# The attention loop of a two-block kernel: maxima by pieces, transposes and value product a step later, the projection begun around the loop's end

## The reference

```python
def diff_attention(q, k_all, v_all, lam):
    s = jnp.einsum('bhmqd,bhmkd->bhmqk', q, k_all).astype(jnp.float32) * ATTN_SCALE
    pr = jax.nn.softmax(s, axis=-1)
    a = pr[:, :, 0] - lam * pr[:, :, 1]
    return jnp.einsum('bhqk,bhke->bhqe', a.astype(v_all.dtype), v_all)

def diff_post(o, p, lam_init):
    o = rmsnorm(o, p['subln_w'], SUBLN_EPS) * (1.0 - lam_init)
```

## Time and profile before

| | |
|---|---|
| Median of three runs | 3520.77 us (3517.88 to 3523.02) |
| Profiled execution | span 3522.8 us, 57651 instructions |
| PE, DVE, ACT busy | 3351.5, 1923.6, 947.3 us (95%, 55%, 27%) |
| Mean granted TensorE clock | 0.977 of full speed |
| Softmax stage, first scores to spill landed | 248.9 to 510.4 us |
| Project stage from | 510.6 us |

### The profile page before, as it was taken

How to read it: one execution, slowest core, us unless ns; L and a number is a source line. 1 busy time by engine, 2 the same in 40 slices (tenths; PEclk the granted TensorE clock), 3 DMA queues, 4 the chain that set the end, 5 groups by cost and what they waited for, 6 DMA issues and landing times.

```text
span 3522.8 us, 57651 instructions
## 1 busy us (share of the span) xinstructions
PE 3351.5 (95%) x25613; PEld 2091.0 (59%) x25613; DVE 1923.6 (55%) x3171; ACT 947.3 (27%) x1914; POOL 51.0 (1%) x117
## 2 busy tenths in 40 slices
PE   7998879989999998989999999999999999999998
PEld 3446655558989887444444444445566447777853
DVE  2137744547767676645655640126988765434524
ACT  3246641115454554211000000100111413233310
POOL 2000000000000000000000000000000000000000
PEclk8999989989989999999999999999999999999999
DMA  6010002300000001232111121113011111100021
GB/s 242 0 55 1 1 25 90 131 30 7 15 18 4 3 3 63 80 102 72 66 49 35 45 98 42 55 48 110 13 52 38 55 66 54 36 24 25 1 90 66
DMA packets 110572, 177.18 MB, mean 50 GB/s; under 512 B 5427, under 2 KB 66482, under 8 KB 109682
## 3 DMA queue, kind: packets, MB, share of 16 engines
q1 hardware_dynamic: 101682, 144.67, 12.1%
q10 hardware_dynamic: 8640, 28.82, 2.4%
HBM read 147.26 MB, written 26.21 MB: 49 GB/s over the span
## 4 chain that ended last, share of the span: by engine, by line
PE 84%; DVE 9%; ACT 4%; DMA 2%; issue 1%; POOL 0%; ACTq 0%; DVEq 0%; SPq 0%; POOLq 0%
PE psum_all L66 82%; ACT sbuf_all L72 3%; DVE sbuf_all L91 3%; DVE sbuf_all L99 2%; DVE sbuf_all L81 2%; PE psum_all L111 1%; ACT L72 1%; DMA sbuf_all<-in_x 1%; DVE sbuf_all L105 1%; DMA sbuf_all<-in_w_out 0%; DVE sbuf_all L88 0%; DMA sbuf_all<-in_w_up 0%; POOL sbuf_all L81 0%; DVE sbuf_all L111 0%; DMA yd_spill<-sbuf_all 0%
## 5 line engine op out<-in xcount | busy, mean ns | idle before, releaser
L66 PE MATMUL psum_all<-sbuf_all 64*64 64x64 f32 (+8 forms) x24858 | 3253.0, 317 | 129.4 <-ACT sbuf_all L72 61.6
L66 PEld LDWEIGHTS psum_all<-sbuf_all 64*64 64x64 f32 (+2 forms) x24858 | 2006.6, 155 | 1351.8 <-issue 966.8
L72 ACT ACTIVATE sbuf_all<-psum_all 128x256 f32<-128x256 f32 (+6 forms) x889 | 363.4, 426 | 1395.5 <-PE psum_all L66 1252.8
L91 DVE SCALAR_TENSOR_TENSOR sbuf_all<-sbuf_all 128x520 f32<-128x520 f32 (+8 forms) x783 | 581.0, 776 | 16.9
L81 DVE TENSOR_TENSOR sbuf_all<-sbuf_all 128x512 f32<-128x512 f32 (+12 forms) x559 | 460.4, 848 | 172.4 <-ACT sbuf_all L72 128.9
L72 ACT ACTIVATE sbuf_all<-sbuf_all 128x64 f32<-128x64 f32 (+16 forms) x539 | 306.7, 581 | 822.6 <-DVE sbuf_all L75 348.6
L75 DVE COPY sbuf_all<-psum_all 128x256 f32<-128x256 f32 (+6 forms) x141 | 72.5, 524 | 456.7 <-PE psum_all L66 430.5
L72 ACT ACTIVATE sbuf_all<-psum_all,sbuf_all 128x1280 f32<-128x1280 f32 (+5 forms) x212 | 164.2, 780 | 312.4 <-PE psum_all L66 273.9
L81 DVE TENSOR_TENSOR sbuf_all<-sbuf_all,psum_all 128x512 f32<-128x512 f32 (+2 forms) x160 | 101.9, 639 | 250.4 <-PE psum_all L66 249.1
L105 DVE COPY_PREDICATED sbuf_all<-sbuf_all,psum_all 128x256 f32<-128x256 int32 (+2 forms) x296 | 143.9, 490 | 68.0 <-PE psum_all L66 62.4
L87 DVE TENSOR_SCALAR sbuf_all<-sbuf_all 128x256 f32<-128x256 f32 (+9 forms) x151 | 57.6, 419 | 163.2 <-ACT sbuf_all L72 160.0
(11 more groups left out here) (21 smaller groups left out, 167.4 us busy)
## 6 DMA issues: line engine op xcount, KB each, us to landing
sbuf_all<-in_w_mod SPq DMA_DIRECT2D x12, 2048.0 KB, 8.0
sbuf_all<-in_w_up SPq DMA_DIRECT2D x22, 1024.0 KB, 7.7
sbuf_all<-in_w_in SPq DMA_DIRECT2D x6, 2048.0 KB, 9.2
x_spill<-sbuf_all SPq DMA_DIRECT2D x16, 512.0 KB, 2.9
sbuf_all<-in_conv_w_in SPq DMA_DIRECT2D x16, 512.0 KB, 5.2
sbuf_all<-in_gla_w_in SPq DMA_DIRECT2D x8, 1024.0 KB, 5.2
sbuf_all<-in_w_down SPq DMA_DIRECT2D x4, 1792.0 KB, 7.5
hid_spill<-sbuf_all ACTq DMA_DIRECT2D x9, 512.0 KB, 2.6
```

Of the source, the lines that this page charges most:

```text
L66: return self.e.matmul(out, lhsT, rhs, start=start, stop=stop, skip_group_check=True)
L72: return self.e.activation(out, in_, func, bias=bias, scale=scale, **kw)
L91: return self.e.scalar_tensor_tensor(out, a, s, b, op0, op1) if self.e is not None else Unissued()
```

## The change

In the softmax stage:

- Scores of both maps lie side by side in PSUM columns 0 to 2559, five banks; bank 5 holds the third transposed group and the value product, banks 6 and 7 the first two groups. The six score matmuls come in the order D, A, E, C, F, B, one signal each. C shares bank 2 with D and waits for it.
- The maxima are taken by these pieces, in the order A, E, D, C, F, B, with a maximum over three values at the end of each map. Map 1 is done first and exponentiated first.
- The transposes are those of step n - 2 and the value product that of step n - 3, and the product comes first. Probabilities of map 0 have three buffers, the transposed ones a single one. ScalarE makes all three copies; VectorE none.
- VectorE does the maxima of step n ahead of the combination of step n - 1. Mean and scalings of a head come four steps later, and all head transposes and outputs leave the loop: five of eight go to TensorE's step 32, three into project_tensor.
- project_tensor waits neither for the end of the softmax stage nor for the spill. It runs head transposes, low-rank products and the last value product in turns. The other engines wait as before.

The diff, with most of the removed lines left out, since they stand above:

```diff
@@ -577,15 +577,16 @@
-    K.pbuf = [[sb.take(ALL) for m in range(2)] for _ in range(2)]
-    K.pT = [sb.take(ALL) for _ in range(2)]
-    K.stats = sb.take(16)
+    K.p0, K.p1 = [sb.take(ALL) for _ in range(3)], [sb.take(ALL) for _ in range(2)]
+    K.pT = sb.take(ALL)
+    K.stats = sb.take(4 * 16)
-    K.small = K.slots([K.ps[:, i * BANK:(i + 1) * BANK] for i in (6, 7)])
-    K.scores = [K.ps[:, 0:ALL], K.ps[:, 3 * BANK:3 * BANK + ALL]]
-    K.score_done = [K.new_signal(f"softmax_score{m}_done") for m in range(2)]
+    K.scores = [K.ps[:, 0:ALL], K.ps[:, ALL:2 * ALL]]
+    K.turn_bank = {0: K.ps[:, 6 * BANK:7 * BANK], 4: K.ps[:, 7 * BANK:8 * BANK], 8: K.ps[:, 5 * BANK:5 * BANK + 256]}
+    K.weigh_bank = K.ps[:, 5 * BANK + 256:5 * BANK + 384]
+    K.score_done = K.new_signal("softmax_score_done")
...
@@ -701,6 +702,15 @@
+SCORES = {"D": (1, 0, 256), "A": (0, 0, 512), "E": (1, 256, 768), "C": (0, 1024, ALL), "F": (1, 768, ALL), "B": (0, 512, 1024)}
+TOPS = (("A", "A", 3), ("E", "E", 0), ("D", "C", 1), ("C", "C", 4), ("F", "F", 2), ("B", "B", 5))
+def softmax_stats(K, n):
+    return K.stats[:, 16 * (n % 4):16 * (n % 4) + 16]
...
@@ -711,52 +721,66 @@
         if n:
             te.wait_ge(*A.s.by("exp", n - 1, 0))
             te.wait_ge(*A.s.by("exp", n - 1, 1))
...
+        for part, (m, a, b) in SCORES.items():
+            rows = slice(m * HEAD, (m + 1) * HEAD)
+            if part == "C":
+                te.wait_ge(*K.score_done.by(n, "D"))
+            te.matmul(K.scores[m][:, a:b], K.q[rows, h, i * P:(i + 1) * P],
+                      K.k[rows, h, a:b]).then_inc(*K.score_done.tick(n, part))
+    def turns(n):
         te.wait_ge(*A.v.by("combined", n))
...
+        for g, bank in K.turn_bank.items():
+            w = min(4, 10 - g)
+            if n:
+                te.wait_ge(*A.s.by("turned", n - 1, g))
+            for kk in range(w):
+                done = te.transpose(bank[:, kk * P:(kk + 1) * P], K.p0[n % 3][:, (g + kk) * P:(g + kk + 1) * P], K.ident)
+            done.then_inc(*A.t.tick("turns", n, g))
     def weigh(n):
         h, i = WORK[n]
...
+        te.wait_ge(*(A.s.by("weighed", n - 1) if n else A.s.by("lam_exp")))
+        te.wait_ge(*A.s.by("turned", n, 8))
+        product(te, K.weigh_bank, lambda kk: pT[:, kk * P:(kk + 1) * P], lambda kk: v[:, kk, h * P:(h + 1) * P],
                 10).then_inc(*A.t.tick("weigh", n))
...
+    last = len(WORK) - 1
+    for n in range(last + 3):
+        if n <= last:
             scores(n)
         if n == 0:
             te.wait_ge(*A.v.by("lam_products"))
...
+            te.matmul(K.weigh_bank[:, 0:2], K.ones, K.lam[:, 0:2]).then_inc(*A.t.tick("lam"))
+        if n > 2:
+            weigh(n - 3)
         if n > 1:
...
+            turns(n - 2)
+        if n == last + 1:
+            te.wait_ge(*A.s.by("exp", last, 0))
+            te.wait_ge(*A.s.by("exp", last, 1))
+            K.bank.turn = -1
+            for x in range(5):
+                turn_head(K, te, *divmod(x, 2))
+def turn_head(K, te, h, g):
+    A = K.softmax
+    te.wait_ge(*A.v.by("normed", h, g))
+    bank = open_bank(K, te, "yd", h, g)
+    for i in range(4):
+        done = te.transpose(bank[:, i * P:(i + 1) * P], K.o_rows[:, h, 4 * g + i, :], K.ident)
+    done.then_inc(*A.t.tick("yd", h, g))
+def last_weigh(K, te):
+    A, n = K.softmax, len(WORK) - 1
+    te.wait_ge(*A.s.by("weighed", n - 1))
+    te.wait_ge(*A.s.by("turned", n, 8))
+    product(te, K.weigh_bank, lambda kk: K.pT[:, kk * P:(kk + 1) * P], lambda kk: K.v[:, kk, 3 * P:4 * P],
+            10).then_inc(*A.t.tick("weigh", n))
 def softmax_vector(K, ve):
@@ -773,37 +797,29 @@
         ve.tt(neg_lam, lam[:, 3:4], lam[:, 2:3], ALU.subtract).then_inc(*V.tick())
         ve.wait_ge(*V.now())
         ve.ts(neg_lam, neg_lam, -LAM_INIT, ALU.add).then_inc(*V.tick())
+    def tops(n):
+        s_ = softmax_stats(K, n)
+        for part, written, col in TOPS:
+            m, a, b = SCORES[part]
+            ve.wait_ge(*K.score_done.by(n, written))
+            ve.reduce(s_[:, col:col + 1], K.scores[m][:, a:b], ALU.max).then_inc(*V.tick())
+            if part in "FB":
+                at = 3 - 3 * m
+                ve.wait_ge(*V.now())
+                ve.reduce(s_[:, 6 + m:7 + m], s_[:, at:at + 3], ALU.max, negate=True).then_inc(*V.tick("top", n, m))
+    def combine(n):
+        s_ = softmax_stats(K, n)
+        ve.wait_ge(*A.s.by("exp", n, 0))
+        ve.wait_ge(*A.s.by("exp", n, 1))
+        if n >= 4:
+            ve.wait_ge(*A.s.by("weighed", n - 4))
+        ve.recip(s_[:, 10:12], s_[:, 8:10]).then_inc(*V.tick())
         ve.wait_ge(*V.now())
...
+        ve.stt(s_[:, 12:13], s_[:, 11:12], neg_lam, s_[:, 8:9], ALU.mult, ALU.mult).then_inc(*V.tick())
         ve.wait_ge(*V.now())
...
+        ve.stt(K.p0[n % 3], K.p1[n % 2], s_[:, 12:13], K.p0[n % 3], ALU.mult, ALU.add).then_inc(*V.tick("combined", n))
     def head_mean(h):
         ssq = K.ssq[:, h * NT:(h + 1) * NT]
...
@@ -822,27 +838,25 @@
     def head_out(h, g):
         ve.wait_ge(*A.t.by("yd", h, g))
-        ve.ts(K.q[:, h, g * 512:(g + 1) * 512], K.small.view("yd", h, g), K.col["subln_w"], ALU.mult, 1.0 - LAM_INIT,
+        ve.ts(K.q[:, h, g * 512:(g + 1) * 512], K.bank.view("yd", h, g), K.col["subln_w"], ALU.mult, 1.0 - LAM_INIT,
               ALU.mult).then_inc(*V.tick())
-        K.small.end(("yd", h, g), V.now())
+        K.bank.end(("yd", h, g), V.now())
     for n in range(len(WORK) + 1):
-        h, step = n // 8 - 1, n % 8
+        h, step = (n - 12) // 8, (n - 12) % 8
+        if n < len(WORK):
+            tops(n)
         if n == 1:
             negative_lam()
+            ve.wait_ge(*V.now())
         if n:
             combine(n - 1)
-        if h >= 0 and step in (5, 6):
-            head_out(h, step - 5)
-        if n < len(WORK):
-            top(n, 0)
-            top(n, 1)
-        if n:
-            turned(n - 1, 8)
-        if h >= 0 and step == 2:
+        if h >= 0 and step == 0:
             head_mean(h)
-        if h >= 0 and step in (3, 4):
-            head_rows(h, step - 3)
+        if h >= 0 and step in (1, 2):
+            head_rows(h, step - 1)
+    for x in range(6):
+        head_out(*divmod(x, 2))
     head_mean(3)
     for g in range(2):
         head_rows(3, g)
@@ -856,33 +870,33 @@
     for s in K.heads_.ends():
         se.wait_ge(*s)
     se.wait_ge(*A.t.by("lam"))
...
+    se.activation(K.lam[:, 2:4], K.weigh_bank[:, 0:2], ACT.Exp).then_inc(*S.tick("lam_exp"))
     def exp(n, m):
...
+        s_ = softmax_stats(K, n)
         se.wait_ge(*A.v.by("top", n, m))
...
+        if m == 0 and n >= 3:
+            se.wait_ge(*A.t.by("turns", n - 3, 8))
+        if m == 1 and n >= 2:
             se.wait_ge(*A.v.by("combined", n - 2))
...
+        to = K.p1[n % 2] if m else K.p0[n % 3]
+        se.activation(to, K.scores[m], ACT.Exp, bias=s_[:, 6 + m:7 + m], accum=s_[:, 8 + m:9 + m]).then_inc(*S.tick("exp", n, m))
+    def turned(n):
+        if n:
+            se.wait_ge(*A.t.by("weigh", n - 1))
+        for g, bank in K.turn_bank.items():
+            w = min(4, 10 - g)
+            se.wait_ge(*A.t.by("turns", n, g))
+            se.activation(K.pT[:, g * P:(g + w) * P], bank, ACT.Copy).then_inc(*S.tick("turned", n, g))
     def weighed(n):
         h, i = WORK[n]
...
         o = K.o_rows[:, h, i, :]
         se.wait_ge(*A.t.by("weigh", n))
...
+        if n + 1 < len(WORK):
+            se.wait_ge(*A.t.by("turns", n + 1, 8))
+        se.activation(o, K.weigh_bank, ACT.Copy, scale=softmax_stats(K, n)[:, 10:11]).then_inc(*S.tick("weighed", n))
         se.wait_ge(*S.now())
         se.activation(K.sq_junk, o, ACT.Square, accum=K.ssq[:, h * NT + i:h * NT + i + 1]).then_inc(*S.tick("squared", n))
@@ -891,20 +905,18 @@
         se.wait_ge(*A.v.by("mean_square", h))
         se.activation(ssq, ssq, ACT.Sqrt).then_inc(*S.tick("root", h))
-    for n in range(len(WORK) + 2):
-        if 0 < n <= len(WORK):
-            turned(n - 1, 0)
-            turned(n - 1, 4)
+    for n in range(len(WORK) + 4):
+        if 3 <= n < len(WORK) + 3:
+            turned(n - 3)
+        if n >= 4:
+            weighed(n - 4)
         if n < len(WORK):
+            exp(n, 1)
             exp(n, 0)
-            exp(n, 1)
-        if n > 1:
-            weighed(n - 2)
-        if n >= 10 and n % 8 == 2:
-            head_root(n // 8 - 1)
+        if n >= 12 and n % 8 == 4 and n < len(WORK) + 1:
+            head_root(n // 8 - 1 if n < 36 else 3)
     head_root(3)
-    for s in (A.t.final(), A.v.final()):
-        se.wait_ge(*s)
+    se.wait_ge(*A.v.final())
     se.dma_start(K.yd_dram, K.q).then_inc(*K.dma("spill_yd").tick())
@@ -940,8 +952,6 @@
 def project_tensor(K, te):
     J, hT = K.project, K.hT
-    for s in (*K.softmax.ends(), K.dma("spill_yd").final()):
-        te.wait_ge(*s)
     def turn_values(j):
         te.wait_ge(*J.v.by("conv", 2, j))
@@ -962,11 +972,25 @@
         done.then_inc(*J.t.tick("mod_sum", block))
```

(22 more changed lines are left out.)

77 lines of the change are left out of this document (removed).

## The result

| | before | after |
|---|---|---|
| Median, timed side by side | 3521.89 us (4 runs, 3517.88 to 3525.95) | 3489.85 us (4 runs, 3488.88 to 3495.29) |
| Ratio | | 0.9909, 95% interval 0.9895 to 0.9922 |
| Span of the profiled execution | 3522.8 us | 3493.1 us |

A forecast was written before the change was run, and what follows sets the result against it. It took TensorE, busy for 95% of 3522.8 us, as the bound, so time saved ahead of the projection counts. Loop 5.7 plus tail 10.1 made 15.8 us, giving 3505.0 us against the median; range 3497 to 3516.

The forecast's parts named there:

- The ring of the step: Attention loop: chain from scores through maxima and exponentials back to scores, forecast at 7.07 us a step instead of 7.11.
- exponentials 1.53 + 1.42: Loop step on ScalarE: 1.53 us from first exponential to second, then 1.42 to the accumulator read.
- 0.15 to TensorE: End of the loop step: 0.15 us from ScalarE's accumulator read to TensorE's next scores.
- lower bound for the step: Attention loop: cheapest case, small maximum 0.05 less and A ready at 0.95, giving a step of 6.9 us.
- Heads: Loop steps that carry a head's end: 2.5 us extra for three heads where 7.0 were, a gain of 4.5.
- Start: Slow first three steps of the loop: 3.0 us extra left as before, between 1 and 5.
- The tail: From last scores to low-rank products done: 54.8 us against 64.9, 10.1 earlier.
- Pieces at full hand-over: Maxima in the loop: each piece costs the full 0.11 us hand-over, step 7.84, program 3529 us; 5%.
- Less overlap: Maxima in the loop: pieces overlap by 0.03 us instead of 0.08, program 3511 us; 14%.
- Scores in strict order: Score matmuls in the loop run in program order, A ready 0.15 us later each step, program 3510 us; 5%.
- Hidden tail: Projection keeps its old end as TensorE meets late copies or sums; only the loop's 5.7 us left, 3515 us; 8%.
- The case without low clock: No low clock in the tail and a start of 1 us, program 3500.5 us; 15%.

The follow-up runs named there:

- b_bothtops: The kernel before, with the first exponential made to wait for both maxima; 3564.49 us.
- b_onewait: The kernel before, with a step's scores waiting only for the second exponential (map 1) of the step before; 3513.5 us.
- a_twowait: The kernel after, with scores waiting for the exponentials in the order they are made (map 1, then map 0), so the second is its own wait; 3502.33 us.
- a_again: The kernel after once more, unchanged; 3491.29 us.
- b_nospill: The kernel before, with TensorE's part of the projection not waiting for the landing of the spill; 3516.03 us.
- a_combfirst: The kernel after, with VectorE doing the combination of step n - 1 ahead of the maxima of step n; 3512.57 us.
- a_oldtail: The kernel after, with low-rank products beginning only when the whole softmax stage has ended and the spill has landed; 3506.41 us.
- a_shift7: The kernel after, with a 512-column low-rank product at the start of the projection done twice; 3507.74 us.
- a_whole: The kernel after, with one whole maximum per map instead of pieces, both exponentials waiting for both; 3566.32 us.

## Why the prediction was wrong in size

**The ring of the step: right in structure, two terms mis-sized.** Up to the first exponential the working holds to 0.03: A ready early, pieces 0.61 and 0.33 apart (five from 375.80 to the small maximum at 378.38), small maximum, hand-over. The failed terms are the last two. "exponentials 1.53 + 1.42" took a start-to-start time of ScalarE from a place where it ended on a wait; 1.32 is the pace (b_bothtops). "0.15 to TensorE" took a hand-over with two waits for one that the change made single; it is 0.05 (b_onewait, a_twowait). In the sum the first term is 0.21 too long and the second 0.10. With 0.03 and 0.01 from the rest that is 0.35 a step, 31 x 0.35 = 10.9 us; the start below takes 1.9 of it back and the heads give 0.2: 9.2. Its lower bound for the step, 6.9, varied only the pieces and didn't hold the 6.72.

**Heads: right.** 7.50 for a long step, +0.78 each for three, 2.3 where 2.5 were forecast.

**Start: 3.0 us forecast, 4.9 measured** (215.5 - 31 x 6.72 - 2.3). From 248 to 283 us the granted clock is 0.90 in before, 0.76 in this profile of after and 0.90 in a_again, whose loop is 2.1 us shorter: the size lies within what one kernel shows from run to run.

**The tail: right in sum, the reason half right.** 54.4 for 54.8. But I spread the gain over work drawn forward, and b_nospill's tail gets nearly all of it from the one wait for the spill. The late spill cost TensorE nothing: ScalarE stood idle for 14 us ahead of its first low-rank copies at 505.31, and TensorE never waited for them.

**The rest:** 0.9 from the opening and 3.4 behind the projection, both in unchanged code. Both stretches differ between two profiles of the same kernel too: a_again has its first exponential 1.3 later than after, and takes 1.2 less behind the mark, a part that took from 2805 to 2823 us in these kernels. No run ties these 4.3 us to the change. I had left them out and had no range for them. Together 9.2 + 0.4 + 0.9 + 3.4 = 13.9, which is 29.7 less 15.8.

**The rivals.** Pieces at full hand-over: refuted by pieces 0.61 apart. Less overlap: the Trainium skill, "VectorE: DVE Perf Modes", section on the TRN2 errata, with its table's price of 120 + n cycles for a PSUM read (its sentence on small tiles speaks of SBUF latency), would space them 0.66 and 0.39 (an estimate); the trace has 0.61 and 0.33, so back-to-back pieces don't pay that price in full from start to start. Scores in strict order ("TensorE: Matmul & The Clock Gate", section "The mechanism", of the Trainium skill): A would have been read from 1.28 on; VectorE starts at 1.17, nearer to the 1.13 of halves side by side. Hidden tail: refuted by 212 of 212 busy us. The case without low clock was the nearest in number only; with its step of 6.95 it set the lower end, 3497, and was still 7 short, and its mechanism did not come: the start took 4.9 us and not 1, and the tail had 3.4 us of low clock.

## What to carry to other kernels

A start-to-start time is a price only where nothing was waited for in between: look up what ended just before the second start, and take the value from a step where the wait was over before (here step 0 of the same loop had it). When a change turns the order of producers round, look at the order of the waits as well: waiting first for what comes last makes the others free. And compare changes of a few us by stages up to a common instruction, since one later stage of the same instructions took anything from 147.7 to 157 us in the profiles here.

## What the runs showed of the hardware

- A second wait of TensorE on ScalarE's counter, for a value that came 1.3 us or more after the first, cost 0.09 us at the start of the matmul (0.14 in a_twowait against 0.05 in after; 0.15 in before against 0.06 in b_onewait). Which of the two waits is written first decides whether it is paid.
- One stage of identical instructions took 147.7 us with 3.4 us at the low clock (a_combfirst, a_oldtail, b_onewait) and 157.0 us with 24 us of it (a_shift7): 0.45 us for each us of it. The same program repeated on one chip spread over 13 us (a_again).
- Back-to-back maxima over 1280 PSUM columns start 1.41 us apart though each is shown as 1.49 long (a_whole, two in 2.89 us); where the second waits for the first's result it is 1.60 (before, two in 3.09 us).
